# Feed-forward products of a fused two-block layer: seven quarter products in place of eight, with the sums on GpSimd and VectorE

## The reference

```
h2 = modulate(rms_norm_2(x, ffn_pre_g[l]), sh2, sc2)
x = x + g2 * rms_norm_2(sq_relu_mlp(h2, w_ff1[l], w_ff2[l]), ffn_post_g[l])
# sq_relu_mlp(h, w1, w2) = square(relu(h @ w1)) @ w2
```

## Time and profile before

| | us |
|---|---|
| median of 3 runs | 3055.98 (3050.77 to 3057.98) |
| span of the profiled execution, first to last instruction | 3054.6 |
| layer 0 feed-forward, units 1 to 15 on TensorE, until layer 1's first product | 1966.4 to 2400.1 |
| layer 1 feed-forward, units 1 to 15 on TensorE | 2837.9 to 3046.3 |

### The profile page before, as it was taken

One profiled execution on the slowest core, in us unless ns is written; L12 is line 12 of the kernel. 1 busy time (PEld: TensorE's weight loads), 2 busy tenths in 40 slices (PEclk: granted clock), 3 DMA queues, 4 the chain that ended last, 5 costly groups with the idle time before them and its releaser, 6 DMA issues.

```text
span 3054.6 us, 31208 instructions
## 1 busy us (share of the span) xinstructions
PE 2906.2 (95%) x12164; PEld 1720.5 (56%) x12164; DVE 1270.1 (42%) x3060; ACT 457.2 (15%) x919; POOL 83.1 (3%) x111
## 2 busy tenths in 40 slices
PE   4989999999999999999899999999999999999998
PEld 3565455445554454444487588544444677587764
DVE  6764112444441021111378846573491268731101
ACT  1222001222211010000112131110000111311100
POOL 0000000000000000000000001000000000000000
PEclk9979999999999999999999999999999999999999
DMA  8558999999999999999853324342441343134342
GB/s 332 226 206 345 372 388 383 404 382 400 395 388 394 404 366 398 394 406 399 362 207 138 138 83 175 129 179 96 151 165 55 122 154 138 56 116 160 120 158 94
DMA packets 110497, 762.08 MB, mean 249 GB/s; under 512 B 12976, under 2 KB 13360, under 8 KB 21776
## 3 DMA queue, kind: packets, MB, share of 16 engines
q1 hardware_dynamic: 94464, 695.25, 57.4%
q0 software_dynamic: 8816, 50.07, 4.3%
q10 hardware_dynamic: 7072, 14.76, 1.3%
HBM read 749.81 MB, written 10.22 MB: 249 GB/s over the span
## 4 chain that ended last, share of the span: by engine, by line
PE 82%; DMA 10%; DVE 5%; ACT 1%; issue 1%; DVEq 0%; SPq 0%; ACTq 0%
PE ps L545 27%; PE ps L557 17%; DMA ring<-stream 10%; PE ps L779 8%; PE ps L978 7%; PE ps L870 7%; PE ps L775 3%; PE ps L1184 2%; PE ps L1172 1%; PE ps L577 1%; PE ps L606 1%; PE ps L880 1%; PE ps L619 1%; DMA area<-modulation 1%; DVE area L1250 1%
## 5 line engine op out<-in xcount | busy, mean ns | idle before, releaser
L545 PE MATMUL ps<-area,ring 128*128 128x256 f32 (+1 forms) x3328 | 820.0, 408 | 0.3
L545 PEld LDWEIGHTS ps<-area,ring 128*128 128x128 f32 x3328 | 632.5, 190 | 183.6 <-issue 108.1
L557 PE MATMUL ps<-ring,area 128*128 128x512 f32 x1216 | 527.8, 595 | 4.0 <-DVE area L2274 4.0
L870 PE MATMUL ps<-ring,area 128*64 128x512 f32 x2112 | 478.0, 598 | 37.8 <-DMA ring<-stream 37.5
L557 PEld LDWEIGHTS ps<-ring,area 128*128 128x128 f32 x1216 | 231.8, 191 | 290.5 <-issue 284.9
L870 PEld LDWEIGHTS ps<-ring,area 128*64 128x64 f32 x2112 | 142.0, 136 | 371.3 <-issue 265.8
L779 PE MATMUL ps<-area,ring 128*128 128x256 f32 x1152 | 255.4, 380 | 0.0
L779 PEld LDWEIGHTS ps<-area,ring 128*128 128x128 f32 x1152 | 216.0, 190 | 28.4
L978 PE MATMUL ps<-ring,area 128*64 128x512 f32 x1024 | 227.2, 596 | 0.0
L2026 DVE SCALAR_TENSOR_TENSOR area<-area,cols 128x256 f32<-128x256 f32 x480 | 201.7, 483 | 1.1
L1591 DVE SCALAR_TENSOR_TENSOR cst<-area,cond,cst 128x256 f32<-128x256 f32 x448 | 183.1, 484 | 0.0
(11 more groups left out here) (344 smaller groups left out, 2055.2 us busy)
## 6 DMA issues: line engine op xcount, KB each, us to landing
ring<-stream SPq DMA_DIRECT2D x638, 1024.0 KB, 8.7
area<-shared_modulation POOLq DMA_DIRECT2D x32, 1024.0 KB, 5.1
area<-modulation SPq DMA_DIRECT2D x16, 1536.0 KB, 6.5
expert_rows<-area ACTq DMA_DIRECT2D x62, 128.0 KB, 7.2
area<-stream POOLq DMA_DIRECT2D x4, 1024.0 KB, 15.3
x<-x_tiles ACTq DMA_DIRECT2D x1, 1024.0 KB, 13.0
area<-ctx_tiles ACTq DMA_DIRECT2D x1, 1024.0 KB, 4.7
input_rows<-area ACTq DMA_DIRECT2D x4, 256.0 KB, 11.8
```

The source lines that it names most:

```text
L545: i = mm(ps[:, b, 0:n], w[:, k % 4, j * P:(j + 1) * P], rhs(k), start=(k == 0), stop=(k == 4 * kgs - 1))
L557: i = mm(ps[:, b, :], lhs(k, t), w[:, k % 4, :], start=(k == 0), stop=(k == 4 * kgs - 1))
L870: i = mm(ps[half(h), bank, :], xT[:, k % 4, half(k // 4)], w[:, 2 * (k % 2) + h, :], start=False, stop=(k == KD - 1))
```

## The change

Units 1 to 15 of both layers are done by Strassen's scheme in Winograd's form, one level deep. Input features, output features and tokens are each cut in two, so a unit's product is a 2 by 2 by 2 product of quarters, and seven quarter products with sums before and behind them take the place of eight. Unit 0 stays as it was. The order of the units is now: ff1 1 to 3, ff2 4 to 7, ff1 8 to 11, ff2 12 to 15 (a unit with `second(i)` is of ff2; two such units add up in the same PSUM banks, `group`), and w_ff2's chunks lie in the stream in that order.

- TensorE does the products in the order 1, 2, 3, 6, 7, 5, 4 (`product`). In layer 0 each has eight matrix products of 256 columns; in layer 1 eight of 128 (ff1) or four of 256 (ff2). Banks are claimed by turns out of all eight.
- Weight sums of 4 x 256 columns: the third (`("weights", i, 3)`) on GpSimd, in place in the ring slot; the second and first on VectorE in `weight_sums`, one unit ahead; the fourth in `last_weight_sum`, into the buffer that product 6 has used.
- Token sums (`sum_tokens`) on VectorE in eight of the units, three or four additions each, 1024 columns in layer 0 and 512 in layer 1.
- ScalarE copies product 1 out of PSUM into `partial`; VectorE adds the others in the `combine_` and `end_` functions (512 columns in layer 0, 256 in layer 1). ScalarE then does Relu and Square in place.
- The modulation chunks from m = 32 on are summed for one condition only. All 24 use one buffer (`late_buffer`), and the load of m + 1 waits for m. VectorE does 18 of their steps in an ff1 unit and 27 in an ff2 unit. A step is one multiplication, or one transposition with its reduction.
- The last two units put products 7 and 4 of both behind the rest, so that the x rows (layer 0) or the first token tile (layer 1) can be finished meanwhile.

The diff, cut to its core:

```diff
+FFU = 16
+ORDER = (1, 2, 3, 6, 7, 5, 4)
+ENDING = 14
+def second(i):
+    return i // 4 % 2
+def group(i):
+    return i | 1 if second(i) else i
+FRESH = (1, 4, 5, 12, 13)
+SUMMED = (1, 4, 5, 7, 8, 12, 13, 15)
+STEPS_IN = {i: 27 if second(i) else 18 for i in range(1, 14)}
+FOLD_AT = {9: 3, 11: 3 + 1, 15: 3 + 2}
...
+        def late_buffer(m):
+            return modsm[m % 2] if m < HALF else modsl[m % 2] if m < MODS else modsl[0]
...
+                def product(i, p):
+                    n = N if l == 0 else P
+                    first, last_ = not second(i) or i % 2 == 0, group(i) == i
+                    key = (L, "part", group(i), p)
+                    b = claim("all", key) if first else bank_of[key]
+                    c = CH["ff1", l, 0] + 2 * i
+                    if p in (1, 2):
+                        chunk(c + p - 1)
+                    if p == 1 and second(i):
+                        pe.wait_ge(*at((L, "hid", hidden_by(i))))
+                    if p in (3, 5, 6, 7):
+                        m = {3: 4, 5: 1, 6: 2, 7: 3}[p]
+                        pe.wait_ge(*at((L, "tokens", summed_at(i, m), m)))
+                    if p in (4, 5, 6, 7):
+                        m = {4: 4, 5: 1, 6: 2, 7: 3}[p]
+                        pe.wait_ge(*at((L, "weights", i, m)))
+                    w, a = weights_of(l, i, p), moved(l, i, p)
...
+                for i in range(1, ENDING):
+                    if i == 4:
+                        spread(1)
+                    fold(i)
+                    for p in ORDER:
+                        product(i, p)
+                for i in (ENDING, ENDING + 1):
+                    fold(i)
+                    for p in (1, 2, 3, 6, 5):
+                        product(i, p)
+                for i in (ENDING, ENDING + 1):
+                    for p in (7, 4):
+                        product(i, p)
+                if l == 0:
+                    turned_rows(("L1", "h"), ("L1", "xn"), 0, TT)
...
             def modulation_steps(m, w, part2, part2t):
+                conds = 2 if m < MODS + MODG else 1
                 for k in range(KD):
-                    for s in range(2):
+                    for s in range(conds):
...
+                def weight_sums(i):
+                    c = CH["ff1", l, 0] + 2 * i
+                    low, high = slots(l, i)
+                    for n in (c, c + 1):
+                        dve.wait_ge(landed[n % RING], 16 * (n // RING + 1))
+                    if i > 2:
+                        dve.wait_ge(*at(("chunk", c - 3)))
+                    dve.wait_ge(*at((L, "weights", i, 3)))
+                    TT_(turned2[i % 2], low[:, :, 256:512], low[:, :, 0:256], ALU.add)
+                    dve.wait_ge(*at((L, "weights", i, 2)))
+                    TT_(turned1[i % 2], high[:, :, 256:512], turned2[i % 2], ALU.subtract)
+                def last_weight_sum(i):
+                    dve.wait_ge(*at((L, "made", i, 6)))
+                    dve.wait_ge(*at((L, "weights", i, 1)))
+                    TT_(turned2[i % 2], turned2[i % 2], slots(l, i)[1][:, :, 0:256], ALU.subtract)
...
+                weight_sums(1)
+                sum_tokens(1)
+                for i in range(1, FFU):
+                    ending = group(i) == i
+                    if ending:
+                        combine_first(i)
+                    if i + 1 < FFU:
+                        weight_sums(i + 1)
+                    if l == 0:
+                        if i in FOLD_AT:
+                            take_sums(FOLD_AT[i], None)
+                        for _ in range(STEPS_IN.get(i, 0)):
+                            next(later, 0)
+                    last_weight_sum(i)
+                    if i == FFU - 1:
+                        continue
+                    if ending:
+                        combine_second(i)
+                        combine_third(i)
+                        end_second(i)
+                        end_third(i)
+                    if i + 1 in SUMMED:
+                        sum_tokens(i + 1)
+                    if ending:
+                        end_last(i)
+                combine_second(FFU - 1)
                 if l == 0:
                     coefficients(1, (0, 1, 2))
+                end_second(FFU - 1)
+                add_to_x(range(nf // 2))
+                combine_third(FFU - 1)
+                end_third(FFU - 1)
+                end_last(FFU - 1)
+                if l == 0:
+                    modulated(("L1", "h"), [(0, TT, 0)], 0)
+                add_to_x(range(nf // 2, nf))
...
                 def load_sums(m):
                     if m > LATE + 1:
-                        pool.wait_ge(*at(("part2", m - 2)))
-                    pool.dma_start((modsm if m < HALF else modsl)[m % 2], mods2_d[m])
+                        pool.wait_ge(*at(("part2", m - 1 if m > MODS else m - 2)))
+                    pool.dma_start(late_buffer(m), mods2_d[m])
...
+                if l == 0:
+                    load_sums(MODS)
+                for i in range(1, FFU):
+                    c = CH["ff1", l, 0] + 2 * i
+                    low, high = slots(l, i)
+                    for n in (c, c + 1):
+                        pool.wait_ge(landed[n % RING], 16 * (n // RING + 1))
+                    nc.gpsimd.tensor_tensor(low[:, :, 256:512], high[:, :, 256:512], low[:, :, 256:512], ALU.subtract)
+                    for m in summed_in().get(i - 1, ()) if l == 0 else ():
+                        if m + 1 < LAYERS * MODS:
+                            load_sums(m + 1)
```

More of the change, by code:

```diff
@@ L2241, in _, with later_steps @@
                 diagonals(1)
[L2242 to L2251, removed]
[L2252 to L2264 removed]
+                def later_steps():
+                    for m in range(MODS, LAYERS * MODS):
+                        dve.wait_ge(*landing(m))
+                        yield from modulation_steps(m, late_buffer(m), part2l, part2lt)
@@ new lines, in onto, with combine_first @@
+                def onto(i, t, o, part, *keys, op=ALU.add):
+                    dst = ends(l, i, t, o)
+                    if second(i) and i > 8:
+                        plus(dst, dst, part, *keys[:1], op=op)
+                        plus(dst, dst, sum_of(i), *keys[1:])
+                    else:
+                        plus(dst, sum_of(i), part, *keys, op=op)
+                def combine_first(i):
+                    part = taken(i, 2)
+                    dve.wait_ge(*at((L, "first", i)))
+                    onto(i, 0, 0, part, free(i, 2), (L, "ended", i, 0, 0))
@@ new lines, in squares @@
+                def squares(key, src):
+                    A(junkb, src, ACT.Square, accum_out=stat((key, "ssq"))).then_inc(*mark("squares_summed", ("ssq", key)))
+                    act.wait_ge(*last("squares_summed"))
+                for j in range(4):
+                    key = ((L, "ff1", 0), j)
+                    act.wait_ge(*at(("full", key)))
+                    squared(hid[:, j, 0:NF], ps[:, B(key), 0:NF], ("drained", key))
+                for n, i in enumerate(GROUPS):
+                    if i == 5:
+                        spread(1)
+                    act.wait_ge(*at((L, "made", i, 1)))
+                    if n >= 2:
+                        act.wait_ge(*at((L, "ended", GROUPS[n - 2], 1, 0)))
+                    A(like(l, i, partial[n % 2]), like(l, i, ps[:, B((L, "part", i, 1)), :]), ACT.Identity).then_inc(
+                        *mark("products_copied", ("drained", (L, "part", i, 1)), (L, "first", i)))
+                    if not second(i):
+                        for t, o in ((0, 0), (0, 1), (1, 1), (1, 0)):
+                            act.wait_ge(*at((L, "ended", i, t, o)))
+                            squared(ends(l, i, t, o), ends(l, i, t, o), (L, "rectified", i, t, o), *([(L, "hid", i)] if (t, o) == (1, 0) else []))
@@ new lines, in _ @@
+                for part in range(2):
+                    tiles = range(nf // 2 * part, nf // 2 * part + nf // 2)
+                    for o in range(2):
+                        act.wait_ge(*at((L, "ended", FFU - 1, part, o)))
+                    for t in tiles:
+                        squares(((L, "y", 1), t), yb[:, t, :])
+                    for t in tiles:
+                        root(((L, "y", 1), t), 1)
+                    for t in tiles if l + 1 < LAYERS else ():
+                        act.wait_ge(*at((L, "x2", t)))
+                        squares(((f"L{l + 1}", "n1"), t), rowsx[t])
+                    for t in tiles if l + 1 < LAYERS else ():
+                        root(((f"L{l + 1}", "n1"), t), 1)
```

230 lines of the change are left out of this document (152 added, 78 removed).

## The result

The changed kernel takes 3082.2 us (median of 4 runs, 3079.1 to 3085.6) against 3055.5 for the kernel before: ratio 1.0093, 95% interval 1.0078 to 1.0107. It is slower by 27 us, inside the predicted range (3012 to 3090) and on the side that got 0.54, but 16 above the predicted 3066.

The account below looks back on a forecast made before the run. TensorE's work was taken to bound both feed-forward stretches, with VectorE's queue order adding stalls in layer 0: 31 us later there, 21 earlier in layer 1, giving a span of 3064.6 and a median of 3066; range 3012 to 3090.

Parts of the forecast that it names:

- the side that got 0.54: Whole kernel: slower than the band of 3050 to 3062 us that counts as unchanged; chance 0.54.
- TensorE's count: Layer 0: a unit falls from 27.5 to 24.2 us, fifteen units from 412 to 363.
- Queue order and single buffer: Layer 0: last weight sum queued behind modulation steps, which wait for one buffer's loads; stalls of 67.5 us together.
- GpSimd beside VectorE: Layer 0: GpSimd's add delays the last weight sum by 0 to 2.6 us, taken as 0.9 in seven units: 6.
- Clock: Layer 0: half clock on TensorE after each stall over about 4 us, 1.7 us each, seven counted: 12.
- Start, spread and folds, tail: Layer 0: late start 4.4 us, spread and folds 4.5, from last product to next stage 6.4.
- Layer 1: Layer 1's feed-forward stretch: no stall, 192.4 us against 213.6, so 21 earlier.
- A: Whole kernel: the forecast itself, own range 3056 to 3086 us; chance 0.52.
- B: Whole kernel: the clock does not fall and the port costs nothing, 3048 us; chance 0.16.
- D: Whole kernel: VectorE hides wholly and TensorE's count decides, 2982 us; chance 0.06.
- C: Layer 0: modulation loads do not make VectorE wait, stalls some 20 us, kernel 3013; chance 0.12.
- E: Layer 0: GpSimd blocks VectorE its whole add (+12), low clock lasts three products per stalled unit (+15): 3093 us; chance 0.14.

Follow-up runs that it names:

- the kernel with both edits: Three half-chunk buffers, modulation steps behind the unit's own sums, 22 steps a unit (24 in the last), against the changed kernel: 2982.6 us, ratio to before 0.977.
- The two single edits: Each alone against the changed kernel: modulation steps behind the unit's own sums, 3028.9 us; three half-chunk buffers for modulation chunks 24 to 47, 3032.4 us.
- the filler: Changed kernel plus extra TensorE products in the hole before product 4 of layer 0's units 8 to 12: 3071.3 us.
- the late diagonals: On the kernel with both edits, VectorE's gate diagonals made behind unit 1's weight and token sums: 2978.1 us, ratio to before 0.975.
- the kernel without reloads: Changed kernel without the loads of modulation chunks 25 to 47 and VectorE's waits for them: 3021.1 us.

## Why the prediction was right, and what was mis-sized

By its own steps, layer 0:
- **TensorE's count.** 24.2 a unit and 363 for fifteen: confirmed (24.17 in the kernel with both edits).
- **Queue order and single buffer.** 67.5 predicted, 67.1 measured. The eight holes before product 4 are 80.8, of which 13.7 is what the nine last weight sums of units 5 to 13 take over 1.22 each (24.7 in all, below); 67.1 are left. The two single edits and the two together show that each cause makes about half of the loss, and that neither edit alone removes it. By units the holes less the port's share are 7.1, 13.3, 5.2 to 5.6 four times, 10.3 and 15.2, for 6.9, 13.2, 5.0, 12.3 and 15.1 predicted; unit 12's is 2.0 shorter because unit 11's slow product is hidden in it.
```profile
L2408 DVE TENSOR_TENSOR area<-area,ring 128x1024 f32<-128x1024 f32 x9 | 24.7, 2749 | 0.3
```
- **GpSimd beside VectorE.** The mis-sized term: 6 predicted, 13.7 measured. I called the start of the two a toss-up and took a third of the bound. It is not one: the load and VectorE's transpose and reduction hang on the same step, so GpSimd's add starts just ahead (0.13 in the rows above), and 2.1 is lost in each of units 7 to 12 and 1.2 in unit 5, where I had put 0.9 in seven. By the Trainium skill ("SBUF — State Buffer", "Who interferes with whom") the port pair that the two share is an exclusive lock, and the order of issue decides who blocks; the trace agrees (3.31 for 1.22, ending 1.09 after GpSimd's 2.35). The upper bound of 2.6 a unit that I had set beside this rule was nearer than my 0.9.
- **Clock.** The other one: 12 predicted (7 stalls of 1.7), 20 measured: the nine groups of eight products behind the holes take 1.8 to 3.1 over 3.62, 20.2 in all. Of these 1.8 are at the start, which I had left out; the eight stalls lose 2.3 each where I had read 1.7 from two holes. Counting one of them out was right: the filler shows that 2.0 was hidden in unit 12's wait. The two terms can thus be read as 67.1 and 20.2, or as 69.1 and 18.2. The filler and the late diagonals show that it is the holes that cost the clock.
- **Start, spread and folds, tail.** 4.4, 4.5, 6.4 predicted; 3.4, 4.4, 7.3 measured. These with 362.6 for the products make 478.7 of 481.2; 2.5 stay unassigned. The later conv gate cost 2.1 with all else between the stretches, for 1; no run separates it.
- **Layer 1.** 192.4 predicted, 191.8 measured twice.
- **Rivals.** The time lies in A's own range (3056 to 3086). B (no loss of clock, no port) and D (TensorE decides) are shown wrong for this kernel; C is what the kernel without reloads is, 3021 for my 3013, and the kernel with both edits comes to 2982.6, close to D's 2982. E's mechanisms are what the two mis-sized terms lean towards: the port close to its upper bound, the low clock for one product, not for three.
- **Signs and readings.** One sign did not come: VectorE is busy for 66% of the stretch (the windows row below), and its slices read 5 to 7, where I had named more than 7 tenths. My own sum (294 of 464) would have given 63%. The 22 us above the 294 are for the most part the stretched last weight sums (17). And in the slices of the kernel before VectorE's share in layer 0's stretch is 1 to 9 tenths, not 2 to 9.
```profile
1961.00:2442.00 481.00, 392.93 (x1760) 337.85 (x1760) 315.62 (x531) 51.52 (x88) 43.35 (x36) 0.91 0.33 120
```

So the direction came from the right cause. Layer 0's stretch is 17.2 longer than the predicted 464, and 15.9 of that are the two mis-sized terms (7.7 and 8.2). That the medians also miss by 16 is partly chance: the span misses by 12.7 only, since the unchanged part ahead was 5.1 shorter in the profiled run. For the port my bounds held and the value was taken too low; for the clock the loss per hole lay inside its bounds (0.8 to 2.5) on average only, 2.2, with 3.1 at most.

## What to carry to other kernels

When a change takes work from one engine and gives a smaller sum to another, don't compare totals: find the last instruction that the next product waits for and add up what stands ahead of it in its queue, waits included. Here nearly the same instructions in another order, with half a chunk more of buffer and an even share of steps, turned a loss of 27 us into a gain of 73. Where two engines are released by the same event and share something, their collision is not chance; price it at its full length.

## What the runs showed of the hardware

- GpSimd's float32 add of 128x1024 takes 2.35 us, twice VectorE's 1.22; VectorE's add that starts 0.13 behind it takes 3.31. A 0.48 us step caught the same way took 2.65. Where VectorE's add came first, GpSimd's, 0.53 behind it, took 2.90.
- A hole on TensorE of about 3 us may or may not be followed by the low clock: behind holes of 2.8 to 3.4 us the next eight products took 3.69 in four cases and 5.20 to 5.38 in nine, over these kernels. The same hole of 2.8 in unit 12 cost it in two of three kernels. None of the holes of 0.6 to 1.5 us cost it, and all of those over 3.4 that a product 4 had before it did.
- TensorE's pitch holds at 0.432 for 256 columns over 224 products on end (x448 records, 96.70 us), with the ring's loads and GpSimd's beside it.
